# Two modulation panels go between the sums of squares of a first layer's norm, and later ones inside the tiles of its down-projection

## The reference, cut to what matters

```python
c_act = jax.nn.silu(c)[:, None, :]
cc_act = jax.nn.silu(c_ctx)
mod = jnp.split(c_act @ w_mod[i] + b_mod[i], 6, axis=-1)     # sh1, sc1, ... of the 256 latent tokens
modc = jnp.split(cc_act @ w_mod[i] + b_mod[i], 6, axis=-1)   # of the 256 context tokens
y = xf * lax.rsqrt(jnp.mean(xf * xf, axis=-1, keepdims=True) + EPS)
z = modulate(rms_norm(h, norm1_w), sh1, sc1) @ w_in          # h * (1 + scale) + shift, then the projection
a, bb, cc, gates = split_cols(z, GROUP_SPLITS)               # a: 672 columns, the down-projection
```

## Time and profile before

| | us |
|---|---|
| median of 3 runs | 3075.92 |
| lowest and highest | 3060.35, 3099.84 |
| the profiled execution | 3065.94 |
| its span, first to last instruction | 3064.1 |
| PE busy in the span | 2795.2 (91%) |
| mean granted TensorE clock | 0.954 of full speed |

### The profile page before, as it was taken

The page is one execution under the profiler, slowest core; times in us unless marked ns, Lnnn a source line. Parts: engine busy times, 40 slices in busy tenths (PEclk is TensorE's granted clock), DMA queues, the critical chain, the costliest instruction groups (busy, mean ns, idle before and its releaser), DMA issues. The chain is left out here.

```text
span 3064.1 us, 52810 instructions
## 1 busy us (share of the span) xinstructions
PE 2795.2 (91%) x20541; PEld 2489.6 (81%) x20541; DVE 1368.7 (45%) x2405; ACT 1217.7 (40%) x1791; POOL 1118.0 (36%) x457
## 2 busy tenths in 40 slices
PE   6899879899989999898899899899889999988998
PEld 4667667688789999566689899899779989977898
DVE  2453533433353433545445533534564353356533
ACT  2322223433244444422245544444444444444443
POOL 0101030132235555110215455454426555542553
PEclk8899989999989999998999999999999999989999
DMA  5464043533346666211416566464325646622463
GB/s 176 133 218 125 5 100 115 172 93 105 97 124 196 186 193 194 66 34 37 103 36 185 166 193 195 144 193 151 97 83 165 200 136 198 188 87 70 144 193 103
DMA packets 570661, 413.55 MB, mean 135 GB/s; under 512 B 36567, under 2 KB 548253, under 8 KB 570525
## 3 DMA queue, kind: packets, MB, share of 16 engines
q1 hardware_dynamic: 570524, 411.69, 45.1%
HBM read 410.58 MB, written 2.88 MB: 135 GB/s over the span
## 5 line engine op out<-in xcount | busy, mean ns | idle before, releaser
L543 POOL TENSOR_TENSOR wlo<-raw,whi 128x768 fp32r<-128x768 f32 (+2 forms) x353 | 1019.7, 2892 | 1670.2 <-ACT whi L534 1669.8
L566 PE MATMUL psum<-xh_n,whi 128*128 128x256 f32 (+1 forms) x3208 | 930.1, 290 | 73.4 <-DVE rtmp L2616 21.9
L567 PE MATMUL psum<-xl_n,whi 128*128 128x256 f32 (+1 forms) x3208 | 912.9, 285 | 0.0
L568 PE MATMUL psum<-xh_n,wlo 128*128 128x256 f32 (+1 forms) x3208 | 912.0, 284 | 0.0
L543 DVE TENSOR_TENSOR wlo<-raw,whi 128x1280 fp32r<-128x1280 f32 (+2 forms) x353 | 533.2, 1511 | 641.9 <-ACT whi L534 641.8
L534 ACT ACTIVATE whi<-raw 128x2048 fp32r<-128x2048 f32 (+2 forms) x353 | 643.5, 1824 | 391.1 <-PE psum L925 170.9
L566 PEld LDWEIGHTS psum<-xh_n,whi 128*128 128x128 f32 x3208 | 615.2, 192 | 107.9 <-issue 51.4
L567 PEld LDWEIGHTS psum<-xl_n,whi 128*128 128x128 f32 x3208 | 617.0, 192 | 4.8
L568 PEld LDWEIGHTS psum<-xh_n,wlo 128*128 128x128 f32 x3208 | 616.3, 192 | 5.5
L923 PE MATMUL psum<-hidh,whi 128*128 128x256 f32 x1232 | 342.5, 278 | 9.2 <-issue 9.2
L925 PE MATMUL psum<-hidh,wlo 128*128 128x256 f32 x1232 | 342.4, 278 | 0.0
(11 more groups left out here) (337 smaller groups left out, 3807.8 us busy)
## 6 DMA issues: line engine op xcount, KB each, us to landing
raw<-in_ffn_w_in SPq DMA_DIRECT2D x176, 512.0 KB
raw<-in_w_in SPq DMA_DIRECT2D x136, 512.0 KB
raw<-in_w_ffn_in SPq DMA_DIRECT2D x132, 512.0 KB
raw<-in_w_mod SPq DMA_DIRECT2D x96, 512.0 KB
raw<-in_ffn_w_out SPq DMA_DIRECT2D x88, 512.0 KB
raw<-in_w_ffn_out SPq DMA_DIRECT2D x66, 512.0 KB
raw<-in_w_out SPq DMA_DIRECT2D x32, 512.0 KB
raw<-in_w_a_o SPq DMA_DIRECT2D x16, 256.0 KB
```

What stands on the lines that cost most here:

```text
L543: eng.tensor_tensor(wlo[slot][:, c0:c1], raw[raw_at[p0] % 3][:, c0:c1], whi[slot][:, c0:c1].bitcast(F32), ALU.subtract).then_inc(sem_, 1)
L566: pe.matmul(dst, sh, mh, start=start and n == 0, stop=False, skip_group_check=True)
L567: pe.matmul(dst, sh, ml, start=False, stop=False, skip_group_check=True)
L568: last = pe.matmul(dst, sl, mh, start=False, stop=n == len(pairs) - 1, skip_group_check=True)
```

## The change

On PE, rows and sum of panels 0 and 1 are taken out of the loop and stand between the matmuls that add the squares: rows 0, two sums of squares, sum 0, rows 1, two sums of squares, sum 1, four sums of squares. In the loop, now j = 1 to 3, the sum of panel 2j and the rows of panel 2j+1 stand after the third tile of k = 2j-2 instead of after the sixth, and the sum of panel 2j+1 ahead of the tiles of k = 2j-1 instead of behind them. On DVE, rows and vectors of panels 0 and 1 come before the reciprocal, and the subtraction of panel j before lo_of instead of behind. On ACT, panel 0 is split right after the square root, and panels 1, 2, 3 after tiles 1, 3, 5 instead of 3, 5, 7. Nothing that is computed changes.

```diff
-        def pe_sum(pe, tag, nk, bk, cols):
+        def pe_sum(pe, tag, nk, bk, cols, ks=None):
-            for k in range(nk):
+            for k in ks or range(nk):
...
-            pe_sum(pe, ("norm1", 0), 8, 6, slice(0, T))
+            pe.wait_ge(*act_done.at("silu c"))
+            mod_rows(0)
+            pe_sum(pe, ("norm1", 0), 8, 6, slice(0, T), range(0, 2))
+            mod_sum(0)
+            mod_rows(1)
+            pe_sum(pe, ("norm1", 0), 8, 6, slice(0, T), range(2, 4))
+            mod_sum(1)
+            pe_sum(pe, ("norm1", 0), 8, 6, slice(0, T), range(4, 8))
             end("pe", "load")
...
-            pe.wait_ge(*act_done.at("silu c"))
-            for j in range(4):
+            pe.wait_ge(*dve_done.at("par"))
+            for j in range(1, 4):
                 mod_rows(2 * j)
-                if j == 1:
-                    pe.wait_ge(*dve_done.at("par"))
-                if j:
-                    open_panel(pe, j - 1)
-                    hi, lo = down_k(2 * j - 2)
-                    for g in range(6):
-                        down_tile(g, 2 * j - 2, hi, lo)
-                mod_sum(2 * j)
-                mod_rows(2 * j + 1)
-                if j:
-                    hi, lo = down_k(2 * j - 1)
-                    for g in range(6):
-                        m = down_tile(g, 2 * j - 1, hi, lo)
-                    m.then_inc(panel_used, 1)
+                open_panel(pe, j - 1)
+                hi, lo = down_k(2 * j - 2)
+                for g in range(6):
+                    down_tile(g, 2 * j - 2, hi, lo)
+                    if g == 2:
+                        mod_sum(2 * j)
+                        mod_rows(2 * j + 1)
                 mod_sum(2 * j + 1)
+                hi, lo = down_k(2 * j - 1)
+                for g in range(6):
+                    m = down_tile(g, 2 * j - 1, hi, lo)
+                m.then_inc(panel_used, 1)
...
+                if l == 0:
+                    split_act(act, 0)
                 for k in range(8):
                     hi_of(k)
-                    if l == 0 and k % 2:
-                        split_act(act, k // 2)
+                    if l == 0 and k in (1, 3, 5):
+                        split_act(act, (k + 1) // 2)
...
-                dve_rstd(dve, tg, slice(0, T))
                 for j in range(4):
                     for m in (2 * j, 2 * j + 1):
                         mod_rows(m)
                         mod_vectors(m)
+                    if j == 0:
+                        dve_rstd(dve, tg, slice(0, T))
                     dve.wait_ge(*dve_done.at(("mod", "vectors", 2 * j + 1)))
                     factors(2 * j, 2 * j + 2)
                     scaled(2 * j)
                     scaled(2 * j + 1)
+                    split_dve(dve, j)
                     lo_of(2 * j)
                     lo_of(2 * j + 1)
-                    split_dve(dve, j)
```

## The result

The kernel before ran beside the changed one: medians 3083.29 us (20 runs, 3060.35 to 3099.84) and 3050.14 us (20 runs, 3030.69 to 3069.11), a ratio of 0.9899 with a 95% interval of 0.9879 to 0.9919. That is 33 us or 1.0% less. The profiled execution took 3051.05, its span 3049.3, with 2807.0 us of PE and a mean granted clock of 0.957.

The account below looks back on a forecast made before the run. PE was taken to be bound by four waits, 22.1 us together, for POOL's half of the weight split, the end of a chain. 27.2 us until T4 plus 2.4 behind it, 29.6 off 3075.92, gave 3046.3 us; range 3024 to 3066.

Parts of the forecast that it names:

- The front: Stretch until the first down-projection matmul: forecast to end at 36.0 instead of 40.76 us, a gain of 4.8.
- The periods: Times between first down-projection matmuls of successive pairs in PE's loop: forecast 13.6, 11.8 and 11.7 us, before 19.39 to 20.16.
- T4: First down-projection matmul of the last pair, forecast at 73.1 us; behind it 14 slow matmuls become fast, 2.4 us kept.
- T1: First down-projection matmul of the first pair, forecast at 36.0 us, before at 40.76.
- the 4.2 us of the other bound: Loads at the front: if all three panels end together, panel 0 arrives at 21 us and everything shifts by 4.2.
- The loads: Down-projection panel loads in the loop: forecast to fit, 11.4 of 13.8 us even with the whole 8 us of landing.
- POOL beside DVE: Shared ports in the loop: POOL could hold up `hn` or `xl` by 1.3 us in each of three periods, gain 25.7.
- The clock stays low: Rival for PE's loop: waits go but the clock stays low, gain 7 us, time 3069; chance 8%.
- Half effect: Rival: only the 22.1 us of waits go, front and clock give nothing, gain 19.7, time 3056; 14% together with load-bound.
- Slower, as the low clock moves elsewhere: Rival for later attention stages: more low-clock spells of 2.8 us each, with fifteen 3088 us; chance 8%.
- the part behind T4 + 8 unchanged in length: Sign for the program after the changed stretch: wrong if the later 2950 us change by more than 10.
- T2: First down-projection matmul of the second pair, forecast at 49.6 us, with granted clock near 1 from there on.

Follow-up runs that it names:

- the run with the early split: Changed kernel with panel 0 copied between the third and fourth squares, subtracted before the reciprocal, and 27 matmuls of zeros in PE's first wait; ratio 0.9914.
- the front alone: Kernel before with only rows and sums of panels 0 and 1 between the sums of squares, and DVE's rows and vectors before the reciprocal; ratio 0.9981.
- the two runs with zeros: Changed kernel with 30 matmuls of zeros in PE's first wait, ratio 0.9932; or with 27 and panel 0 split early, ratio 0.9914.
- the two runs with doubled loads: Changed kernel, down-projection panels 1 to 3: both loads of each done twice, ratio 0.9962; or only the second done twice, ratio 0.9917.
- The run with one load doubled: Changed kernel with only the second of the two loads of down-projection panels 1 to 3 done twice; ratio 0.9917, key norm at 80.3 us.
- the split alone: Kernel before with only the weight splits made sooner on ACT and DVE, PE's order unchanged; ratio 0.9972, key norm at 93.2 us.
- the loop alone: Kernel before with only the new order of sums and rows in PE's loop, front and splits unchanged; ratio 0.9921, key norm at 91.9 us.
- loop and split: Changed kernel with the front of before (panels 0 and 1 behind all eight sums of squares, reciprocal first on DVE); ratio 0.9933, key norm at 83.1 us.
- before again: Kernel before, run once more without an edit; ratio 0.9992, key norm at 110.1 us, span 3096.7 us.
- front and loop: Changed kernel with the splits of before (ACT behind xh, DVE behind xl); ratio 0.9956, key norm at 87.6 us.
- loads doubled: Changed kernel with both loads of down-projection panels 1 to 3 done, waited for and done again; ratio 0.9962, key norm at 87.8 us.

## Why the prediction was right

It gave 3046.3 and -29.6 us; measured were 3050.14, -33 us, and -29.8 us at the key norm. That these lie so close is in part luck. The base of the forecast, 3075.92 from three runs, was 7.4 us below the median of twenty, and the gain of the medians some 3.5 us above the forecast; the two offset each other in part. And the changed part began 0.9 us later in the profile of the changed kernel than in that of before; from L784 its gain is 30.7 us, 1.1 above the forecast: some 0.6 in the front, 0.1 in the periods and 0.4 behind T4. The mechanism, point by point:

- **The front.** T1 came at 36.29, forecast 36.0. The transposes ended at 17.6 and not 16.75, which nothing in the change explains (over the runs they end between 16.5 and 18.2). From rows 0 on it was 18.7 us, forecast 19.25: two errors against each other. Panel 0 I had put at 15, with delay 0; in the run with the early split it is there at 17.28 only (with the front alone rows 0 began at 17.01 without a wait), so the delay is up to 0.6 where the transposes end early. Neither is the 4.2 us of the other bound.
- **The first wait** of 7 us, ended by DVE's `xl`: 7.09.
- **The periods**, forecast 13.6, 11.8 and 11.7: measured 13.62, 11.84 and 11.50. The waits on `wlo` are gone, and the last pair's wait is 0.60.
- **Behind T4** I had kept 2.4 of 2.8 us; 5.65 for 8.44 gives 2.79. Without any slow matmuls the forecast gain would have been some 7 us lower; these rows, and the two runs with zeros, speak for counting them where the trace shows them. The Trainium skill (TensorE: Matmul & The Clock Gate, section "What's actually happening") advises "don't fit to a specific cold count", as the penalty is under 1% of a typical kernel's span. That isn't contradicted, 7 us being 0.2% of this span, but it is a quarter of this gain.
- **The loads.** The conclusion (no wait) was right, its slack wrong: with the whole 8 us of landing I had 2.4 us, but a panel lands 3.9 us after the issue, and the two runs with doubled loads put the slack at some 6.
- **POOL beside DVE.** In the changed kernel the subtraction of panels 1 to 3 is done while DVE is nearly idle, and takes 1.20 us (1.21 in the later two); that of panel 0 (30.31) falls beside DVE's reciprocal, which has one input, and takes 1.19. The run with one load doubled shows the rival: where POOL met `hn`, DVE took 0.97 us more (I had set 1.3). The Trainium skill's lock on the shared pair of ports (SBUF — State Buffer, section "SBUF: two separate sides") fits that and the 2.07 of before, which comes back as soon as both subtract side by side.
- **The rivals.** *The clock stays low* fell: it is 1.00 from T2 on. *Half effect* fell: front, loop and clock all gave. *Slower, as the low clock moves elsewhere*: the late part of the two unchanged profiles took 2946.3 and 2977.5 us, that of the two changed ones 2961.2 and 2959.4. They lie between, so nothing points to a loss there, though two profiles a side can't exclude one of some us.
- **A step that failed:** "the part behind T4 + 8 unchanged in length", with 10 us as the point at which I would be wrong. It differed by 14.9 us between the two profiles. The test was no test: the same kernel differs from itself by 31 us. On the medians nothing speaks against it: the rest averages 2960.9 over the fourteen profiles, and the gains at the key norm, summed over the twelve that have an edit, are 268.6 us, against 249 by the ratios (the twelve shortfalls from 1 add up to 0.0807, times 3080), and each ratio is uncertain by 4 to 13 us.

**What gives the gain.** The parts don't add: front 2.7, split 15.5 and loop 16.8 would be 35, together they give 29.8 (from L784: 36.2 and 30.7). With the split alone, `xl` ends the wait; with the loop alone, `wlo` does; each takes away one of two things that are late. Both are needed for the last 9 us (25.6 for 16.8), because only then the wait drops below zero.
What the front is worth, counted from L784: 3.7 us beside loop and split, 3.7 beside the loop, 3.1 alone, and -0.8 in the one profile beside the split alone, where it brought 2.5 us at T1 and the clock took it back.

## What to carry to other kernels

When PE waits each round for a chain of short steps, price three things together: work moved between the chain's start and its end on PE, steps taken off the chain, and the clock that comes back when the wait goes. The third was worth 2.8 us behind the last wait here and 2 us where zeros kept the clock up, and it blurs the other two as long as waits of 2 to 3 us are left. And read the effect of an early change between two markers, one just ahead of it and one close behind it, not at the end of the span, if the same kernel's spans differ by as much as the effect.

## What the runs showed of the hardware

**The same matmul loop runs at two rates at the same granted clock.** Windows in a long feed-forward stage, of the kernel before, of the same kernel again, and of the changed kernel:
```profile
1780.00:1880.00 100.00, 100.00 (x885) 100.00 (x884) 37.79 (x44) 44.07 (x45) 58.05 (x19) 1.00 0.63 189
```
```profile
1780.00:1880.00 100.00, 100.00 (x852) 100.00 (x851) 36.53 (x42) 42.37 (x42) 54.98 (x19) 1.00 0.61 184
```
```profile
1780.00:1880.00 100.00, 100.00 (x852) 100.00 (x851) 36.60 (x41) 42.16 (x41) 56.59 (x18) 1.00 0.61 186
```
PE is busy throughout with matmuls of 256 columns and the granted clock is 1.00 in all three, yet 885 or 852 start in 100 us: one each 113.0 or 117.4 ns. The timeline shows it in every row, not in gaps. The changed kernel, then the kernel before, near 2950 us:
```profile
2950.20 0.28 PE L927 MATMUL psum<-hidh,whi 128*128 128x256 f32 x1
2950.32 0.28 PE L928 MATMUL psum<-hidl,whi 128*128 128x256 f32 x1
2950.44 0.28 PE L929 MATMUL psum<-hidh,wlo 128*128 128x256 f32 x1
```
```profile
2950.37 0.28 PE L923 MATMUL psum<-hidh,whi 128*128 128x256 f32 x1
2950.48 0.28 PE L924 MATMUL psum<-hidl,whi 128*128 128x256 f32 x1
2950.59 0.28 PE L925 MATMUL psum<-hidh,wlo 128*128 128x256 f32 x1
```
A stage of some 200 us is either fast or slow from end to end. Of the seven such stages between 850 and 3040 us the profile of before had none slow, its repetition four, the changed kernel's two. This goes with the column "rest": the two profiles with no slow stage (before, one load of two doubled) have 2946.3 and 2954.8 us there, the two with four (before again, loads doubled) 2977.5 and 2975.4. From 1562.0 to 2098.0 the changed kernel took 536.0 us, before 527.8 for the same work, and most of that is one slow stage. Another 7.6 us went between 2098.0 and 2145.8 (47.8 us for 40.2). There the granted clock was 0.79 and 0.78, before 0.84 and 1.00, with a wait of 4.1 us at DVE's `xl_n` in both. What picks the rate, or the clock in that stretch, no run here separates; kernels with and without the change show both.

**Behind waits of 2.4 to 2.9 us the clock went either way.** This is read from PE's waits in the changed part alone. Behind those of up to 1.6 us ahead of a pair's first matmul the clock was never seen to fall. Behind those of 3.7 us or more it always fell, but not always at once: in the profile before, the sum behind 3.72 us still starts fast and the next one is slow.
```profile
30.02 0.61 PE L759 MATMUL psum<-cst,mrows 128*128 128x2 f32 x4 [3.72 <-DVE mrows L2048]
...
33.01 1.01 PE L759 MATMUL psum<-cst,mrows 128*128 128x2 f32 x4 [0.53 <-DVE mrows L2048]
```
Between these lie two waits of 1.85 and 1.90 us at which the clock was low already, and waits of 2.43 to 2.92 us, behind which it went either way: of four waits of 2.75 us one left it up, one had it low at once, and two let it fall within 1.3 us of the restart; 2.43 us (loop alone, and front and loop, the last pair) had it low, 2.92 us (loads doubled, the last pair: 5.64 us until the key norm) left it up. I had not expected waits of one length to differ by this; it makes up to 2.5 us at one pair.
